# Second feed-forward block: nine of its twenty-two first-layer weight slots by Strassen's scheme of seven half-size products

## The reference, cut to what matters

```python
def swiglu(u, w_in, w_out):
    gate, up = jnp.split(u @ w_in, 2, axis=-1)
    return (jax.nn.silu(gate) * up) @ w_out
...
        u = modulate(rms_norm(h, norm_ffn[layer]), sh2, sc2)
        h = h + g2[:, None, :] * swiglu(u, ffn_w_in[layer], ffn_w_out[layer])
```

## Time and profile before

| | us |
|---|---|
| runs of the kernel | 2142.99, 2143.0, 2135.43 (median 2142.99) |
| the profiled execution, first to last instruction (span) | 2142.1 |
| TensorE busy in it | 2069.3 (97%) |
| VectorE busy | 1286.0 (60%) |
| ScalarE busy | 892.2 (42%) |
| GpSimd busy | 263.3 (12%) |
| mean granted TensorE clock | 0.988 of full |

### The profile page before, as it was taken

One profiled execution on the slowest core, in us unless ns is written; L12 is line 12 of the kernel. 1 busy time (PEld: TensorE's weight loads), 2 busy tenths in 40 slices (PEclk: granted clock), 3 DMA queues, 4 the chain that ended last, 5 costly groups with the idle time before them and its releaser, 6 DMA issues.

```text
span 2142.1 us, 26418 instructions
## 1 busy us (share of the span) xinstructions
PE 2069.3 (97%) x10328; PEld 1758.7 (82%) x10328; DVE 1286.0 (60%) x1900; ACT 892.2 (42%) x1259; POOL 263.3 (12%) x280
## 2 busy tenths in 40 slices
PE   7999999999999999999999999998999998999997
PEld 3888888888888888866788888886688887888886
DVE  7877766454544562586545444588547766565656
ACT  5533343475656645466422222255134343322222
POOL 3000000054444413010000000001400000000000
PEclk9999999999999999999999999999999999999998
DMA  6642231445555533321132233222013222222321
GB/s 222 222 171 99 99 119 47 151 158 205 189 196 201 200 129 118 118 72 48 59 118 99 99 103 114 99 82 81 32 65 108 93 95 79 99 99 99 101 97 39
DMA packets 39484, 247.50 MB, mean 116 GB/s; under 512 B 4927, under 2 KB 5183, under 8 KB 11588
## 3 DMA queue, kind: packets, MB, share of 16 engines
q1 hardware_dynamic: 27940, 191.75, 25.8%
q0 software_dynamic: 8080, 47.79, 6.5%
q10 hardware_dynamic: 3344, 6.29, 0.8%
HBM read 239.52 MB, written 6.29 MB: 115 GB/s over the span
## 4 chain that ended last, share of the span: by engine, by line
PE 83%; DVE 8%; issue 3%; ACT 2%; POOL 2%; DVEq 0%; ACTq 0%; POOLq 0%
PE bank L762 24%; PE bank L763 23%; PE bank L764 23%; PE bank L1105 2%; DVE w_lo L2123 2%; ACT w_hi L1592 1%; PE bank L962 1%; PE bank L1233 1%; PE bank L1243 1%; PE bank L1254 1%; PE bank L801 1%; PE bank L942 1%; DVE scr L2196 1%; POOL pool L717 0%; ACT pool L1580 0%
## 5 line engine op out<-in xcount | busy, mean ns | idle before, releaser
L762 PE MATMUL bank<-u_hi,w_hi 128*128 128x512 f32 x1656 | 649.8, 392 | 13.9 <-DVE w_lo L2123 6.1
L763 PE MATMUL bank<-u_lo,w_hi 128*128 128x512 f32 x1656 | 630.7, 381 | 0.0
L764 PE MATMUL bank<-u_hi,w_lo 128*128 128x512 f32 x1656 | 630.5, 381 | 0.0
L2123 DVE TENSOR_TENSOR w_lo<-raw,w_hi 128x2048 fp32r<-128x2048 f32 x160 | 368.0, 2300 | 191.0 <-ACT w_hi L1592 190.7
L1592 ACT ACTIVATE w_hi<-raw 128x2048 fp32r<-128x2048 f32 x160 | 304.5, 1903 | 271.2 <-PE bank L764 258.0
L762 PEld LDWEIGHTS bank<-u_hi,w_hi 128*128 128x128 f32 x1656 | 315.1, 190 | 72.2 <-issue 17.4
L764 PEld LDWEIGHTS bank<-u_hi,w_lo 128*128 128x128 f32 x1656 | 314.8, 190 | 45.1
L763 PEld LDWEIGHTS bank<-u_lo,w_hi 128*128 128x128 f32 x1656 | 315.1, 190 | 44.7 <-issue 3.3
L762 PE MATMUL bank<-g_hi,w_hi 128*128 128x512 f32 x768 | 294.7, 384 | 6.4 <-DVE w_lo L2123 4.5
L763 PE MATMUL bank<-g_lo,w_hi 128*128 128x512 f32 x768 | 291.8, 380 | 0.0
L764 PE MATMUL bank<-g_hi,w_lo 128*128 128x512 f32 x768 | 291.6, 380 | 0.0
(11 more groups left out here) (311 smaller groups left out, 2307.9 us busy)
## 6 DMA issues: line engine op xcount, KB each, us to landing
raw<-in_wts SPq DMA_DIRECT2D x180, 1024.0 KB, 4.9
pool<-in_wts POOLq DMA_DIRECT2D x36, 1024.0 KB, 5.2
spectra<-pool ACTq DMA_DIRECT2D x16, 256.0 KB, 2.1
scr<-in_rel POOLq DMA_DIRECT2D x16, 256.0 KB, 3.1
pool<-spectra POOLq DMA_DIRECT2D x16, 256.0 KB, 3.1
H<-in_x ACTq DMA_DIRECT2D x1, 2048.0 KB, 14.8
out<-H SPq DMA_DIRECT2D x8, 256.0 KB, 2.0
pool<-in_window POOLq DMA_DIRECT2D x1, 1024.0 KB, 9.1
```

The source lines that it names most:

```text
L762: pe.matmul(out, lh, rh, start=start, stop=False, skip_group_check=True)
L763: pe.matmul(out, lh, rl, start=False, stop=False, skip_group_check=True)
L764: return pe.matmul(out, ll, rh, start=False, stop=stop, skip_group_check=True)
L2123: dve.tensor_tensor(w_lo[RING[w]][:, :], raw[W_STREAM[w] % raw_ring][:, :], w_hi[RING[w]][:, :].bitcast(F32), ALU.subtract).then_inc(lo_do ...
```

## The change

**TensorE.** fi5, fi7, ... fi21 (nine slots) are computed by Strassen's scheme in its Winograd form. The slot's weights are cut into four quarters (a21, a22, a11, a12: two halves of the contraction by gate and up columns), the activations into quarters by halves of the contraction and halves of the tokens. Seven products of half size in each direction replace eight: `FORMS` names their weight side (three quarters of the weights as they are, four sums). Each is 4 chunks x 3 matmuls of 256 moving columns, 84 matmuls for the slot (`slot_fast`). They accumulate in banks 4 to 7, with waits for the engines that read those banks in between.

**GpSimd.** Once, behind the norm, `half_sums` forms the four sums of activation quarters with ten operations of 1024 elements, in order, from `u_hi` and `u_lo`. Then, for each of the nine slots, `weight_sums` forms the four sums of weight quarters, four operations of 512 elements, from the slot's `raw` tile, when that has landed and the units of the previous fast slot have been split.

**ScalarE and VectorE.** Once, behind slot fi2, they split the activation sums in six pieces (two of 1024 elements, four of 512: `upper_half_sum`, `lower_half_sum`). For each fast slot they split seven units of 512 elements in place of one slot of 2048 (`upper_unit`, `lower_unit`). In `fast_slot` ScalarE makes two copies out of banks, two silu of 256 elements and the usual `g_hi`; VectorE makes five additions of 256 elements that combine the products, and two multiplications of 256 in place of one of 512. `FEEDS` places the split of the following fo slot ahead of these.

**SyncE.** A `raw` tile that held a fast slot is loaded again when its seven units are split, not when one `w_lo` is done.

The core of the diff:

```diff
+FAST_FROM = 4
+FAST_BANK = 4
+UNITS = 7
+FORMS = ("a11", "s2", "s3", "s1", "a12", "a22", "s4")
+SUMS = ("s1", "s3", "s2", "s4")
...
+def is_fast(label, i):
+    return label == "fi1" and i >= FAST_FROM and i % 2 == 1
...
+        t_sum = [f_six[:, 0:1024], scr_words[:, 0:1024], scr_words[:, 1024:2048], scr_words[:, 2048:3072]]
+        t_tmp = scr_words[:, 3072:4096]
...
+                    if kind == "W" and W_LIST[n] in FAST_AT:
+                        sp.wait_ge(fu_lo, len(FORMS) * (FAST_AT[W_LIST[n]] + 1))
+                    elif kind == "W":
+                        sp.wait_ge(lo_done, STD_COUNT[n])
...
+            def half_sums():
+                fours = lambda t: t.rearrange("p (k a b) -> p k a b", k=4, a=2)
+                t1, t2, t3, t4 = (fours(x) for x in t_sum)
+                tmp = fours(t_tmp)
+                uh, ul = u_hi[:, :, :].bitcast(F32), u_lo[:, :, :].bitcast(F32)
+                pl.wait_ge(u_l, U_FFN1 + KC)
+                pl.tensor_tensor(t1, quarter(uh, 0, 1), quarter(uh, 0, 0), ALU.subtract)
+                link(pl.tensor_tensor(tmp, quarter(ul, 0, 1), quarter(ul, 0, 0), ALU.subtract))
+                link(pl.tensor_tensor(t1, t1, tmp, ALU.add))
+                link(pl.tensor_tensor(t2, quarter(uh, 1, 1), t1, ALU.subtract))
+                pl.tensor_tensor(t2, t2, quarter(ul, 1, 1), ALU.add).then_inc(ft_sum, 1)
+                pl.tensor_tensor(t3, quarter(uh, 1, 1), quarter(uh, 0, 1), ALU.subtract)
+                link(pl.tensor_tensor(tmp, quarter(ul, 1, 1), quarter(ul, 0, 1), ALU.subtract))
+                pl.tensor_tensor(t3, t3, tmp, ALU.add).then_inc(ft_sum, 1)
+                pl.wait_ge(ft_sum, 1)
+                link(pl.tensor_tensor(t4, quarter(uh, 1, 0), t2, ALU.subtract))
+                pl.tensor_tensor(t4, t4, quarter(ul, 1, 0), ALU.add).then_inc(ft_sum, 1)
+            def weight_sums(n):
+                s = W_STREAM[W_AT[FAST_LIST[n]]]
+                pl.wait_ge(raw_in[s % raw_ring], 16 * (s // raw_ring + 1))
+                if n == 0:
+                    pl.wait_ge(ft_lo, 2)
+                else:
+                    pl.wait_ge(fu_lo, len(FORMS) * n)
+                a21 = raw[s % raw_ring][:, :].rearrange("p (k c) -> p k c", k=KC)[:, 0:4, 0:P]
+                pl.tensor_tensor(source(n, "s1"), a21, source(n, "a22"), ALU.add).then_inc(fs_sum, 1)
+                pl.tensor_tensor(source(n, "s3"), source(n, "a11"), a21, ALU.subtract).then_inc(fs_sum, 1)
+                pl.wait_ge(fs_sum, 4 * n + 1)
+                pl.tensor_tensor(source(n, "s2"), source(n, "s1"), source(n, "a11"), ALU.subtract).then_inc(fs_sum, 1)
+                pl.wait_ge(fs_sum, 4 * n + 3)
+                pl.tensor_tensor(source(n, "s4"), source(n, "a12"), source(n, "s2"), ALU.subtract).then_inc(fs_sum, 1)
+            half_sums()
+            for n in range(len(FAST_LIST)):
+                weight_sums(n)
...
+            def slot_fast(label, i):
+                n = FAST_AT[(label, i)]
+                to = {"a11": 0, "a12": 0, "s2": 1, "s3": 2, "a22": 2, "s1": 3, "s4": 3}
+                waits = {"a11": (f_copy, 2 * n), "s3": (f_comb, 5 * n - 1), "s1": (f_comb, 5 * n),
+                         "a12": (f_copy, 2 * n + 1), "a22": (f_comb, 5 * n + 2), "s4": (f_comb, 5 * n + 3)}
+                for f, form in enumerate(FORMS):
+                    pe.wait_ge(fu_lo, len(FORMS) * n + f + 1)
+                    if form in waits and waits[form][1] > 0:
+                        pe.wait_ge(*waits[form])
+                    if n == 0 and form in ("s2", "s3", "s1", "a22"):
+                        pe.wait_ge(ft_lo, {"s2": 1, "s3": 2, "s1": 6, "a22": 4}[form])
+                    hi, lo = unit_tile(x_unit_hi, f), unit_tile(x_unit_lo, f)
+                    b = bank[FAST_BANK + to[form]][:, 0:256]
+                    opens = form in ("a11", "s2", "s3", "s1")
+                    for k in range(4):
+                        xh, xl = moving(form, k, u_hi, t_hi, t1_hi), moving(form, k, u_lo, t_lo, t1_lo)
+                        pe.matmul(b, hi[:, k, :], xh, start=opens and k == 0, stop=False, skip_group_check=True)
+                        pe.matmul(b, hi[:, k, :], xl, start=False, stop=False, skip_group_check=True)
+                        mm = pe.matmul(b, lo[:, k, :], xh, start=False, stop=k == 3, skip_group_check=True)
+                    complete(mm)
...
+            def upper_unit(n, f):
+                if f == 0:
+                    s = W_STREAM[W_AT[FAST_LIST[n]]]
+                    act.wait_ge(raw_in[s % raw_ring], 16 * (s // raw_ring + 1))
+                if FORMS[f] in SUMS:
+                    act.wait_ge(fs_sum, 4 * n + SUMS.index(FORMS[f]) + 1)
+                if n:
+                    act.wait_ge(product, unit_before(n, f))
+                act.activation(unit_tile(x_unit_hi, f), source(n, FORMS[f]), ACT.Copy).then_inc(fu_hi, 1)
...
+            def upper_half_sum(x):
+                dst, src = t_parts(t_hi, t1_hi)[x]
+                act.wait_ge(ft_sum, min(x, 2) + 1)
+                if x == 4:
+                    act.wait_ge(ft_lo, 4)
+                act.activation(dst, src, ACT.Copy).then_inc(ft_hi, 1)
+            def fast_slot(i, gcount, steps):
+                n = FAST_AT[("fi1", i)]
+                def upper_hidden(x):
+                    act.wait_ge(f_hid, 2 * n + 2)
+                    act.wait_ge(product, used("fo1", x // 2 - 2))
+                    act.activation(g_hi[:, (gcount + x) % NG, :], ff_h[:, x % 2, :], ACT.Copy).then_inc(g_h, 1)
+                feed_steps(steps[0])
+                act.wait_ge(product, PART[len(FORMS) * n])
+                if n == 0:
+                    act.wait_ge(ft_lo, 6)
+                act.activation(f_p1, bank[FAST_BANK][:, 0:256], ACT.Copy).then_inc(f_copy, 1)
+                feed_steps(steps[1])
+                act.wait_ge(f_comb, 5 * n + 3)
+                act.activation(f_act[:, 256:512], f_c22, ACT.Silu).then_inc(f_gate, 1)
+                feed_steps(steps[2])
+                act.wait_ge(product, PART[len(FORMS) * n + 4])
+                act.activation(f_up1, bank[FAST_BANK][:, 0:256], ACT.Copy).then_inc(f_copy, 1)
+                feed_steps(steps[3])
+                act.wait_ge(f_comb, 5 * n + 4)
+                act.activation(f_act[:, 0:256], f_c21, ACT.Silu).then_inc(f_gate, 1)
+                feed_steps(steps[4])
+                upper_hidden(i)
...
+                            if layer == "1" and i == FAST_FROM - 2:
+                                for x in range(6):
+                                    upper_half_sum(x)
...
+            def lower_unit(n, f):
+                dve.wait_ge(fu_hi, len(FORMS) * n + f + 1)
+                dve.tensor_tensor(unit_tile(x_unit_lo, f), source(n, FORMS[f]),
+                                  unit_tile(x_unit_hi, f).bitcast(F32), ALU.subtract).then_inc(fu_lo, 1)
...
+            def lower_half_sum(x):
+                dst, src = t_parts(t_lo, t1_lo)[x]
+                upper = t_parts(t_hi, t1_hi)[x][0]
+                dve.wait_ge(ft_hi, x + 1)
+                dve.tensor_tensor(dst, src, upper.bitcast(F32), ALU.subtract).then_inc(ft_lo, 1)
...
+            def fast_slot(i, steps, lag):
+                n = FAST_AT[("fi1", i)]
+                b1, b2, b3 = (bank[FAST_BANK + x][:, 0:256] for x in (1, 2, 3))
+                in_turn = lambda x: x.rearrange("p (b a) -> p a b", a=2)
+                hidden = ff_h[:, i % 2, :].rearrange("p (a h b) -> p h a b", a=2, h=2)
+                def part(f):
+                    dve.wait_ge(product, PART[len(FORMS) * n + f])
+                feed_steps(steps[0])
+                part(1)
+                dve.wait_ge(f_copy, 2 * n + 1)
+                dve.tensor_tensor(f_u2, b1, f_p1, ALU.add).then_inc(f_comb, 1)
+                feed_steps(steps[1])
+                part(2)
+                dve.wait_ge(f_comb, 5 * n + 1)
+                dve.tensor_tensor(f_u3, b2, f_u2, ALU.add).then_inc(f_comb, 1)
+                lag(i - 1)
+                part(3)
+                dve.wait_ge(f_comb, 5 * n + 2)
+                dve.tensor_tensor(f_c22, b3, f_u3, ALU.add).then_inc(f_comb, 1)
+                feed_steps(steps[2])
+                part(5)
+                dve.tensor_tensor(f_c21, b2, f_u2, ALU.add).then_inc(f_comb, 1)
+                feed_steps(steps[3])
+                part(6)
+                dve.tensor_tensor(f_up2, b3, f_u2, ALU.add).then_inc(f_comb, 1)
+                dve.wait_ge(f_copy, 2 * n + 2)
+                dve.wait_ge(f_gate, 2 * n + 2)
+                dve.tensor_tensor(hidden[:, 0], in_turn(f_act[:, 0:256]), in_turn(f_up1), ALU.mult).then_inc(f_hid, 1)
+                dve.wait_ge(f_comb, 5 * n + 5)
+                dve.tensor_tensor(hidden[:, 1], in_turn(f_act[:, 256:512]), in_turn(f_up2), ALU.mult).then_inc(f_hid, 1)
+                feed_steps(steps[4])
```

## The result

| | before | after |
|---|---|---|
| median of 12 runs each, us | 2135.65 | 2142.03 |
| lowest to highest | 2132.89 to 2143.00 | 2136.84 to 2145.93 |
| ratio, 95% interval | | 1.0024 (1.0013 to 1.0036) |
| profiled execution: own time, span | span 2142.1 | 2141.94, 2139.9 |
| TensorE busy in it, us | 2069.3 | 2062.8 |

The ratio is the 0.24% by which the twelve runs after are slower; its interval, 0.12% either way, leaves out 1, so the change is slower, by 5.1 us. Against its own base it was +0.24%; but it was called no difference, and the terms that made it up were partly wrong.

The account below looks back on a forecast made before the run. TensorE was taken to bound the kernel. The terms -8.6 + 1.9 + 7.9 + 1.7 + 2.4 = +5.3 us on the span of 2142.1 gave 2147.4, so a median of 2148, range 2136 to 2157, called no difference.

Parts of the forecast that it names:

- The short matmuls: Nine fast slots on TensorE: 84 matmuls of 256 columns at 112 ns save 0.95 us a slot, -8.6 us.
- Rival three: Short matmuls are no faster: at 127.5 ns each the first term becomes +3.2 us, total 2160.1; chance 0.07.
- w_lo of fi1: At fi1, VectorE's w_lo is held by one GpSimd addition of the activation sums while TensorE waits: +1.9 us.
- w_lo of fo0: Before fo0, w_lo comes late behind activation sums, pieces and fi5's weight sums taking turns; TensorE waits +7.9 us.
- the door: GpSimd and VectorE instructions with two SBUF inputs exclude each other for a whole instruction, taking turns.
- The clock: Behind the 7.9 us idle at fo0, TensorE's granted clock falls for two 3 us windows: +1.7 us.
- A wait in each fast slot: g_lo, held for the fourth weight sum, delays the fast slot's products: 0.3 us in eight slots, +2.4 us.
- Rival two: Slower: w_lo of the fo slots waits for a whole weight sum, about 1.25 us a slot, 2155.9; chance 0.18.
- Rival one: GpSimd and VectorE holding each other up costs little, only 1.0 us at fo0; gain stays, -7.6, 2135.4; chance 0.20.

Follow-up runs that it names:

- half_sums late: Changed kernel with GpSimd's activation sums started only when w_lo of fi1 is done; measured 1.0036 (1.0023 to 1.0049).
- pieces later: Version with the ten activation sums on VectorE, its lower pieces moved behind fo0's residuals 3 and 5 and the last one; measured 0.9980 (0.9967 to 0.9993).
- no sums: Changed kernel without activation sums and their pieces, fast slots reading plain activation quarters, so output is not the reference's; measured 0.9969 (0.9957 to 0.9981).

## Why the prediction was wrong, and where right

The step that failed is the one from the sum to the statement. "A measurement of this kernel can tell some 0.5%, 10.7 us, from no change" rested on no row. The interval of twelve runs was 0.12% either way, 2.5 us, and so +5.3 us was a forecast of slower, not of no difference. The sum itself came out right (+5.3 forecast, 5.1 by the ratio) by luck: four of its terms were off, two each way. The wait at fo0 was 3.7 us too high and the fast slots 2.4; the clock was 3.9 too low, and the nine slots save 1.1 less.

- **The short matmuls**, -8.6: measured -7.5, some 0.1 us a slot at a22 among it. 112 ns was forecast, 111.7 came; nine slots at 112 ns are 84.7 us, and 85.7 came. The formula that was weighed there (the Trainium skill, page "TensorE: Matmul & The Clock Gate", section "Back-to-back issue gap") gave 109.2, 2.5 ns low for this pattern; the same section says of it that at small N it under-counts, since it leaves out the weight load, and the trace agrees. Rival three falls.
- **w_lo of fi1**, +1.9: measured +1.7 (3.99 for 2.29). Held by one addition, as forecast.
- **w_lo of fo0**, +7.9: measured 4.2, by the same mechanism. Counted from the start of the additions, the sums ended at 30.6 us for the forecast's 33.0 (no piece got between the last two), and w_lo at 41.8 for 43.8, while pieces and weight sums mixed as forecast. TensorE, itself 1.7 us later by the slow clock in fi1, asked later by as much. With the wait and the slow clock at fi1 gone (half_sums late) the wait at fo0 was 8.3. No run takes the door away at fo0 and leaves all else, so how much of the 4.2 is the door and how much the mere length of the chain of sums and pieces is not shown.
- **The clock**, +1.7: too small a term, by the largest error of the four. It counted one fall, behind fo0. The wait at fi1, 3.0 us long, brings one too, 1.7 us each; and in the mean over runs the clock is 5.6 us dearer. The prediction took a clock from a single profiled execution, whose own (0.988) was at the low end of the kernel before (0.988 to 0.993).
- **A wait in each fast slot**, +2.4 (its own steps, 0.13 at u3 and 0.11 more at s4, give 0.24 a slot and 1.9): about 0.1 us a slot, in the -7.5 already. The weight sums began 0.35 us before the slot and not with it, so the third was done when w_lo came, and w_lo came 0.03 us before the fourth. g_lo, held for the fourth sum, cost nothing that TensorE saw. Rival two was that near: in the second trace it happened in one slot, for 1.0 us, and half_sums late has one such wait and pieces later two. That it didn't in all eight is luck, as far as the prediction goes.
- **Rival one**, the gain stays because the door costs little: no. With the sums out of the way (no sums, -7.5) the gain is there, and it is the two waits and what follows them in the clock that take it.

Not settled: of the clock's 0.0029, the two falls shown make some 0.0016 to 0.0021. The rest has no place yet. In the profiled execution of the changed kernel a third fall, 1.7 us again, stands behind a wait of 2.4 us at 1406.83 which the kernel before has too (2.4 at 1411.17) with no fall behind it, and the second trace of the changed kernel has none there either. No run tells why there are more of them in some executions.

## What to carry to other kernels

A gain spread over many slots is small against one preparation put at the wrong place: price the preparation at the point where the critical engine has no slack, and move it to where nothing that this engine waits for stands behind it (pieces behind fi3: 0.9987 and 0.9979 against 1.0024). An engine that is the busier one overall can still have room there: VectorE took all ten sums without holding anybody up. When a wait is moved, ask again what stands behind it: in four of the edits here a wait only changed its place or its name. Waits of TensorE of 3.0 and 4.2 us cost their own length and 1.7 us of clock each. And before calling a forecast "no difference", find out from repeated runs what the measurement can tell.

## What the runs showed of the hardware

- The runs' times lie on a line with their mean granted clock, 1.93 us for 0.001, with 1.2 us left over; executions of one unchanged kernel scatter from 0.988 to 0.993, 2132 to 2144 us, in two clusters (2132.0 to 2136.4 and 2138.6 to 2144.1). Here versions some us apart could be told only over many runs, or at one clock.
- Waits of TensorE of 3.0 and 4.2 us were each followed by the lower clock level, at a loss of 1.7 us; waits of 6.9 and 8.3 us likewise, at a loss of 2.4 and 3.0. Fillers in the place of those of 3.0 and 4.2 kept the clock at 1.00. A wait of 2.9 us was not followed by it; the waits of 2.4 us were in some executions only.
- With GpSimd and VectorE both queueing operands of two SBUF inputs, a GpSimd addition of 2.36 us took up to 4.41 and a VectorE g_lo of 0.69 up to 2.85. Where both waited, they went in turns. Alone, an addition of 1024 took 2.36 us on GpSimd and 1.22 on VectorE.
